# Moving the relative bias product and its two transfers from behind the feed-forward network into its third step

## The reference

```python
h = h + hgrn2_mixer(rmsnorm(h), ...)              # layer one
hn = rmsnorm(h, norm_ffn_g[0])
h = h + (silu(hn @ w_gate) * (hn @ w_up)) @ w_down   # FFN_DIM = 2816: "the network"

# layer two: every attention score gets a bias by distance, from a learned table
tb = rel_bias.T                                   # 16 heads x 32 buckets
lc = einsum(q, k_cmp) + tb[:, rel_bucket(t - cmp_end)]
ls = einsum(q, k_slc) + tb[:, rel_bucket(t - pos)]
lw = einsum(q, k_win) + tb[:, rel_bucket(dist_w)]
```

## Time and profile before

| | us |
|---|---|
| median of 3 runs | 1443.01 |
| lowest and highest run | 1440.4, 1443.49 |
| the profiled execution's own time | 1440.81 |
| its span | 1439.2 |
| PE busy | 1380.9 (96%) |
| DVE busy | 433.9 (30%) |
| ACT busy | 307.4 (21%) |
| POOL busy | 144.5 (10%) |

### The profile page before, as it was taken

One profiled execution on the slowest core, in us unless ns is written; L12 is line 12 of the kernel. 1 busy time (PEld: TensorE's weight loads), 2 busy tenths in 40 slices (PEclk: granted clock), 3 DMA queues, 4 the chain that ended last, 5 costly groups with the idle time before them and its releaser, 6 DMA issues.

```text
span 1439.2 us, 36218 instructions
## 1 busy us (share of the span) xinstructions
PE 1380.9 (96%) x16208; PEld 831.3 (58%) x16208; DVE 433.9 (30%) x646; ACT 307.4 (21%) x495; POOL 144.5 (10%) x215
## 2 busy tenths in 40 slices
PE   7999999999997799999999999999999999999995
PEld 7999999998895583343343343343343343344343
DVE  5985555555567730110110110110110110110120
ACT  5744543434545821000000000000000000000000
POOL 0600100001203705001001001001001001001001
PEclk9999999999997998999999999999999999999998
DMA  9853465557986056999999999999999999999993
GB/s 280 261 168 118 152 202 176 177 189 166 215 242 240 1 206 252 402 418 402 419 418 400 419 418 401 419 418 402 418 418 401 418 419 402 419 418 390 419 399 143
DMA packets 132786, 454.83 MB, mean 316 GB/s; under 512 B 12452, under 2 KB 74109, under 8 KB 132643
## 3 DMA queue, kind: packets, MB, share of 16 engines
q1 hardware_dynamic: 126386, 435.11, 78.0%
q0 software_dynamic: 6080, 17.37, 5.2%
q10 hardware_dynamic: 176, 0.14, 0.0%
HBM read 436.46 MB, written 14.55 MB: 313 GB/s over the span
## 4 chain that ended last, share of the span: by engine, by line
PE 86%; DMA 8%; DVE 3%; ACT 2%; issue 1%; POOL 0%; SPq 0%; POOLq 0%; ACTq 0%; DVEq 0%
PE ps L1647 85%; DMA more<-in_moe_w_gu 4%; DMA ring<-in_moe_w_down 3%; ACT x_hi L926 1%; DMA ring<-in_a_w_in 1%; DVE arena L1492 1%; DVE arena L1489 1%; DMA arena<-item_rows,arena 0%; ACT arena L1134 0%; PE ps L1951 0%; ACT x_hi L956 0%; DVE arena L1493 0%; ACT between L1155 0%; POOL arena L788 0%; PE ps L1759 0%
## 5 line engine op out<-in xcount | busy, mean ns | idle before, releaser
L1647 PE MATMUL ps<-more,arena 128*32 128x448 f32 x3456 | 330.0, 539 | 4.7 <-DMA more<-in_moe_w_gu 4.7
L1616 DVE TENSOR_TENSOR arena<-arena,ps 128x448 f32<-128x448 f32 x48 | 29.8, 621 | 769.6 <-PE ps L1647 765.4
L1647 PE MATMUL ps<-ring,arena 128*32 128x448 f32 x2688 | 258.7, 542 | 1.2 <-ACT arena L1201 1.2
L1647 PEld LDWEIGHTS ps<-more,arena 128*32 128x32 f32 x3456 | 105.1, 110 | 225.4 <-issue 212.1
L1647 PE MATMUL ps<-ring,between 128*32 128x256 f32 x3360 | 189.6, 379 | 0.5 <-DMA ring<-in_moe_w_down 0.4
L1647 PEld LDWEIGHTS ps<-ring,arena 128*32 128x32 f32 x2688 | 82.2, 110 | 168.3 <-issue 158.2
L522 DVE TENSOR_TENSOR w_lo<-ring,w_hi 128x2048 fp32r<-128x2048 f32 x67 | 153.5, 2294 | 77.8 <-ACT w_hi L516 77.7
L1647 PEld LDWEIGHTS ps<-ring,between 128*32 128x32 f32 x3360 | 105.2, 110 | 86.9 <-issue 7.8
L516 ACT ACTIVATE w_hi<-ring 128x2048 fp32r<-128x2048 f32 x67 | 127.6, 1910 | 97.5 <-PE ps L1647 87.9
L1647 PE MATMUL ps<-more,between 128*32 128x256 f32 x2016 | 115.3, 379 | 0.0
L1212 ACT ACTIVATE arena<-ps 128x448 f32<-128x448 f32 x48 | 26.1, 543 | 414.2 <-PE ps L1647 414.2
(11 more groups left out here) (269 smaller groups left out, 1137.0 us busy)
## 6 DMA issues: line engine op xcount, KB each, us to landing
more<-in_moe_w_gu SPq DMA_DIRECT2D x144, 896.0 KB, 20.0
ring<-in_moe_w_gu SPq DMA_DIRECT2D x112, 896.0 KB, 19.5
ring<-in_moe_w_down SPq DMA_DIRECT2D x80, 896.0 KB, 20.0
more<-in_moe_w_down SPq DMA_DIRECT2D x48, 896.0 KB, 20.2
ring<-in_ffn_w_gu SPq DMA_DIRECT2D x22, 1024.0 KB, 5.1
ring<-in_a_w_in SPq DMA_DIRECT2D x16, 1024.0 KB, 11.6
ring<-in_ffn_w_down SPq DMA_DIRECT2D x11, 1024.0 KB, 5.0
ring<-in_w_kv SPq DMA_DIRECT2D x6, 1024.0 KB, 4.9
```

The costliest lines, as they stand in the source:

```text
L1616: dve.tensor_tensor(SU[:, a, :], SU[:, a, :], ps[:, b, 0:QUARTER], ALU.mult).then_inc(bank_free[b], 1)
L1647: return pe.matmul(o, w, x, start=start, stop=stop, **kw)
```

## The change

The constant `BIAS_AT = 2` names the step of the network in which the bias is now computed. TensorE's product stands behind `down(0)` and ahead of `ga` of step 2, in the same bank 0. VectorE's copy stands at the head of step 2, ahead of its read of `ga`. GpSimd's second transfer now stands directly behind the first, ahead of `add_squares(2)`. Nothing else is altered, and no instruction is added or dropped.

```diff
@@ job_table
     for j in range(FFN // 256):
+        if j == BIAS_AT:
+            job(("biasw",), 2 * (j % 2))
         job(("ga", j), 2 * (j % 2))
         job(("up", j), 2 * (j % 2) + 1)
-    job(("biasw",), 0)
@@ GpSimd
             pool.dma_start(scratch.ap().rearrange("p h x -> h p x"),
                            biasrow[:, 0:row].unsqueeze(1).to_broadcast([HB, P, row])).then_inc(rows_out, 16)
-            add_squares(2)
             pool.wait_ge(rows_out, 16)
             pool.dma_start(BD, bass.AP(scratch, P - 1, [[HB * row - 1, P], [row, HB], [1, T]])).then_inc(bias_in, 16)
+            add_squares(2)
@@ VectorE
             for j in range(FFN // 256):
+                if j == BIAS_AT:
+                    k = filled(dve, ("biasw",))
+                    dve.tensor_copy(biasrow, ps[0:HB, k, :]).then_inc(bank_free[k], 1)
                 k = filled(dve, ("ga", j))
...
-            k = filled(dve, ("biasw",))
-            dve.tensor_copy(biasrow, ps[0:HB, k, :]).then_inc(bank_free[k], 1)
             residual("down")
@@ TensorE
             for j in range(FFN // 256 + 1):
+                if j == BIAS_AT:
+                    pe.wait_ge(onehot_loaded, 16)
+                    b = free_bank(pe, ("biasw",))
+                    mm(ps[0:HB, b, :], tb[:, :], OH[:, 0:2 * T], True, True).then_inc(bank_full[b], 1)
                 if j < FFN // 256:
                     project(("ga", j), j == 0)
                     project(("up", j), False)
...
-            pe.wait_ge(onehot_loaded, 16)
-            b = free_bank(pe, ("biasw",))
-            mm(ps[0:HB, b, :], tb[:, :], OH[:, 0:2 * T], True, True).then_inc(bank_full[b], 1)
             project(("kv0", 0), True)
```

More of the change, by code:

```diff
@@ L50 @@
 FK = FFN // P
+BIAS_AT = 2
 HB, G, HP, DH = 16, 4, 4, 64
```

## The result

| | before | changed |
|---|---|---|
| median us | 1443.18 (18 runs) | 1446.47 (18 runs) |
| lowest and highest | 1439.74, 1445.87 | 1443.97, 1449.2 |
| the profiled execution's own time | 1440.81 | 1446.44 |
| its span | 1439.2 | 1444.8 |
| mean granted clock | 0.984 | 0.980 |

The ratio is 1.0024, with a 95% interval of 1.0017 to 1.0032: the change makes the kernel 3.3 us slower, and 2.7 were forecast.

The account below looks back on a forecast made before the run. TensorE's chain, without slack in the network, was taken to bound the kernel. Terms -3.5 + 5.2 + 1.7 - 0.7, with 0 for the stored weights, gave +2.7 on the median 1443.0: 1445.7 us, range 1442 to 1451.5.

Parts of the forecast that it names:

- What bounds the kernel: Whole network: TensorE's unbroken chain of 191.45 us has no slack, so any microsecond it stands there reaches the end.
- Term 1: Network's end: without the bias, TensorE resumes some 2.3 us earlier and the low clock goes, -3.5 us.
- Term 2: Step 2: TensorE's ga waits for bank 0 until VectorE's late bias copy, product included, +5.2 us.
- Term 3: Step 2: TensorE's 4.1 us idle gap drops the clock for about 3.4 us, costing +1.7 us.
- Term 4: Late instruction fetches during the broadcast: two gaps behind the network go (-1.26), some come in it (+0.6), -0.7 us.
- Term 5: Network, after the early broadcast: stored weight halves last until new loads land, so nobody waits, 0 us.
- Rival B: Network: weight queue starves until the second transfer ends, TensorE stands 6.3 us more; sum +9.0, 1452 us; chance 0.14.
- Rival A: Step 2: the clock holds at the upper level despite the wait; sum +1.0, 1444.0 us; chance 0.16.
- rival C: Network: neither clock nor fetches cost anything, only the wait is traded; +0.4 us, 1443.4; chance 0.10.

Follow-up runs that it names:

- the filled gap: Kernel before, plus 19 unread matmuls behind the bias product, filling TensorE's 2.46 us wait at the network's end: 1439.04 us against 1442.68, ratio 0.9978.
- the kernel before with its copy behind: Kernel before, VectorE's bias copy moved behind the addition of the network's output and the lower parts of x: 1436.62 us against 1440.72, ratio 0.9960.
- Bank 2: Changed kernel with the bias product of step 2 written to bank 2, not bank 0: 1438.72 us against 1440.72 of before, ratio 0.9983.
- the copy one split ahead: Changed kernel with VectorE's bias copy one split earlier, ahead of the split for down(1): ratio 1.0004 to the kernel before.
- Putting the transfers back: Changed kernel with GpSimd's transfers alone restored to their old place behind the network, product and copy staying in step 2: ratio 1.0038 to the kernel before.
- the kernel with the product in the first gap: Changed kernel with product in TensorE's 1.1 us wait at the network's start, copy before step 0, transfers from about 163 us: 1439.08 us against 1442.8, ratio 0.9973.

## Why the prediction was right, step by step

- **What bounds the kernel.** Right. TensorE's chain had no slack in the network: the wait of step 2 reappears in full at the end.
- **Term 1, the end of the network** (-3.5). Right in both parts, the start and the clock. From the last matmul of `down(10)` to the second key sweep it is 360.95 - 352.13 = 8.82 us, where it was 355.70 - 343.33 = 12.37 (the last matmul starts at 352.13 and 343.33 in the two timelines): -3.55. The clock's part is shown by the filled gap, the whole by the kernel before with its copy behind (8.80).
- **Term 2, the wait for bank 0** (+5.2). Right. TensorE resumes 5.04 us behind the start of the product, the 1.03 us of the product included; predicted 5.16. Bank 2 shows that the bank makes it, and the copy one split ahead that it is as long as what stands ahead of the copy.
- **Term 3, the clock in that gap** (+1.7). The mechanism was right, the size low: the lower level lasted 6.8 us and not 3.4, and from `ga` of step 2 to the end of the network it is 352.13 - 188.64 = 163.49 us where it was 343.33 - 182.17 = 161.16: +2.33. I took the shorter stretch of the two bounds; with 5.1 busy us in it, half is 2.5.
- **Term 4, the fetches** (-0.7). The sign was right, the size low. From the second key sweep to C it is 35.34 us and was 37.12: -1.78, with both gaps gone and none in the network. Why is open. Putting the transfers back brings a gap back; but of the kernels with late transfers two have no gap there, the one with its gap filled and the one with its copy behind, so moving the transfers is not shown to be what removes them. My reading of the gaps as late instruction fetches fits the traces: each of the eight gaps without a releaser of 0.35 us and more between 150 and 430 us, in six profiles, ends 1.3 to 1.6 us behind the landing of a 16 KB packet of the instruction queue, by the packets' own times. In the profile of before such a packet lies between 364 and 366 us:

```profile
q0 software_dynamic: 44, 0.20, 99.0%
q8 instruction: 1, 0.02, 2.9%
```

Between 331.8 and 364.3 us there is none, where the network otherwise shows one every 12 to 18 us; in the kernel with its copy behind one landed at 348.7, and with the gap filled one at 353.6. But the changed kernel had none between 182 and 215 us and no gap without a releaser. What decides if a late packet stops TensorE, the runs don't separate.
- **Term 5, the weights in store** (0). Right. The loads for `ga` 5, `up` 5 and `down(4)` landed at 228.4, 231.2 and 236.6; predicted 226.5, 229.5 and 241.8. Nobody waited. Rival B is out.
- **Rival A**, the clock holds, is out in three profiles; **rival C** was half right (no fetch gap in the network) but needed A.

The terms, measured, are +5.13 (5.25 from the last matmul of `down(0)` to `ga`, against 0.12), +2.33, -3.55 and -1.78, together +2.1, against +3.3 by the medians. So the total came out near although two of its parts did not: term 3 was 0.6 too small and term 4 took off 1.1 too little, which leaves +2.1, and the other 1.2 of the measured 3.3 belong to no term. The profiles of the two kernels differ by more, 5.6 us in span: 1.3 is the fall at the network's start, and 2.1 lies between C and D, in the attention, where the change alters nothing. TensorE from C to D, before and changed (length, PE busy, granted clock, DMA share, GB/s):

```profile
392.82:546.35 153.53, 133.54 (x1130) 0.91 0.50 168
```

```profile
396.29:551.97 155.68, 135.41 (x1130) 0.90 0.38 134
```

In the three profiles each, TensorE is busy there for 133.5, 134.3 and 133.1 us before and for 135.4, 135.2 and 135.3 changed, with the same matmuls, at a mean clock of 0.91, 0.91 and 0.93 against 0.90 each time. So nearly all of the difference is matmuls that ran longer at the lower level. Why that level lasts longer there in the changed kernel is open. In the profiled executions of before the total was below its median each time (1440.81, 1440.44 and 1441.01 against 1443.18, 1442.8 and 1442.68), so a profile is perhaps not a fair sample of the falls of the clock. That the terms' sum lies 1.2 us from the difference of the medians is as much as can be said.

## What to carry to other kernels

Moving small work out of a handover takes an instant of TensorE at the new place, and either a result bank that the next product doesn't want or a reader that gets there at once. Here a free bank gained (0.9983) with the reader 3.3 us late, while a reader nearly on time with the wanted bank only broke even (1.0004). Read the reader's list ahead of the new place, not its busy share: VectorE was 55% busy here and still 3.3 us late. And before moving anything, try moving the reader behind the urgent work: two lines did at least as much (0.9960) as the whole change with its bank repaired (0.9983; the two intervals just touch).

## What the runs showed of the hardware

- The length of the gap alone doesn't settle whether the lower clock comes: behind 4.0 us of idle time it fell in 4 of 4 profiles, behind 2.46 us in 3 of 3, behind 1.41 us in the one there is, behind 1.09 us at the network's start in 5 of 12 and at its end in 2 of 8. It then lasted 6.8 us behind 4.0 us, 3.4 or 6.8 behind 2.46, and 3.4 behind the shorter ones. In the kernel with the product in the first gap it fell for 3.4 us at the network's start, behind idle times of no more than 0.30 us.
- At the network's start it fell in 0 of 3 profiles of one kernel and in 3 of 3 of another, although the two are the same up to there. Profiles of one kernel may thus agree with each other more than chance would have it; six are too few to show it.
- A transfer that writes 3 MB to HBM from 16 partitions took 95% of the DMA engines' time at about 95 GB/s (2.87 MB in 30 us) and left the weight queue 2.4 to 2.6%, at either place.
- While it ran and just behind it, 16 KB packets of the instruction queue came up to 35 us apart, and TensorE stood without a releaser for 0.35 to 2.29 us, each time until 1.3 to 1.6 us behind such a packet.
